# The last block's head reordered: a short first route, one query unit in two row buffers, one output unit's slot for rows

## The reference, cut to what matters

```python
h = rmsnorm(x, norm1_g) * (1 + sc1) + sh1
q, k, v, u = split(h @ w_in)
mixed = concat([dilated_attention(q, k, v), multiscale_pool(u)]) @ w_out
x = x + g1 * mixed
h2 = rmsnorm(x, norm2_g) * (1 + sc2) + sh2
x = x + g2 * peer_ffn(h2)
return rmsnorm(x, final_g)

def peer_ffn(h):                       # 8 heads, 2 x 128 sub-keys, 16384 experts
    q = h @ w_q                        # 1024 -> 8 heads x 2 x 128
    s = q . sub_keys                   # two times 128 scores for each token and head
    sv, si = top_k(s, 16)              # the 16 best of each half
    cand = sv[0][:, None] + sv[1]      # 256 sums, with id = 128 * si[0] + si[1]
    top_v, eid = top_k(cand, 16)
    gate = softmax(top_v)
    act = gelu(h . expert_u[eid])
    return sum(gate * act * expert_v[eid])
```

## Time and profile before

| what | us |
|---|---|
| median of 3 runs | 1417.58 |
| lowest, highest | 1414.52, 1530.66 |
| the profiled execution's own time | 1416.4 |
| its span, first to last instruction | 1414.6 |
| busy: PE, DVE, POOL, ACT | 1277.5, 818.0, 651.8, 412.3 |

### The profile page before, as it was taken

The page is one execution under the profiler, slowest core; times in us unless marked ns, Lnnn a source line. Parts: engine busy times, 40 slices in busy tenths (PEclk is TensorE's granted clock), DMA queues, the critical chain, the costliest instruction groups (busy, mean ns, idle before and its releaser), DMA issues.

```text
span 1414.6 us, 17530 instructions
## 1 busy us (share of the span) xinstructions
PE 1277.5 (90%) x6312; PEld 788.6 (56%) x6312; DVE 818.0 (58%) x1681; ACT 412.3 (29%) x1030; POOL 651.8 (46%) x643
## 2 busy tenths in 40 slices
PE   9999999999999999999998899958967888777786
PEld 8887686548886777559566556523323333333332
DVE  1766287340666377350448756889797654554545
ACT  1533334201342333121314323332313231212123
POOL 0556667423446766504004354535645455454540
PEclk9999999999999999999999999979999989999999
DMA  9544344634444254543628999999999999999995
GB/s 373 206 164 180 120 165 168 262 131 183 164 180 173 96 233 177 195 176 141 271 86 329 421 417 415 421 421 421 421 421 421 421 423 421 422 422 421 422 421 209
DMA packets 53888, 407.84 MB, mean 288 GB/s; under 512 B 6165, under 2 KB 8618, under 8 KB 11306
## 3 DMA queue, kind: packets, MB, share of 16 engines
q0 software_dynamic: 36864, 268.45, 45.9%
q1 hardware_dynamic: 15850, 137.23, 25.2%
q10 hardware_dynamic: 1088, 1.05, 0.3%
HBM read 404.58 MB, written 1.07 MB: 287 GB/s over the span
## 4 chain that ended last, share of the span: by engine, by line
PE 28%; DMA 24%; DVE 6%; issue 3%; ACT 2%; POOL 1%; ACTq 0%; DVEq 0%; POOLq 0%
PE bank L1119 10%; DMA ring<-in_peer_uv,vM 7%; DMA yT<-in_peer_uv,vM 7%; PE pj L729 6%; PE pj L693 4%; DMA hv<-in_peer_uv,vM 4%; DMA more_rows<-in_peer_uv,vM 3%; DMA qM<-in_peer_uv,vM 3%; PE pj L989 2%; PE pj L708 2%; DVE tri L1871 1%; DMA qvE<-in_peer_uv,vM 1%; PE bank L999 1%; ACT rope L1338 1%; DVE big L1871 1%
## 5 line engine op out<-in xcount | busy, mean ns | idle before, releaser
L693 PE MATMUL pj<-xT,ring 128*128 128x256 f32 (+1 forms) x1568 | 318.4, 363 | 0.9 <-ACT hv L1276 0.4
L693 PEld LDWEIGHTS pj<-xT,ring 128*128 128x128 f32 x1568 | 276.6, 190 | 36.5 <-issue 2.6
L607 POOL TENSOR_SCALAR more_rows<-more_rows,lbt 128x256 f32<-128x256 f32 x168 | 176.0, 1048 | 16.4
L641 POOL DMA_INDIRECT ring<-in_peer_uv,vM x101 | 122.5, 1213 | 120.9 <-PE bank L1119 109.5
L729 PE MATMUL pj<-ring,yT 128*128 128x512 f32 x320 | 141.1, 595 | 0.0
L605 POOL TENSOR_SCALAR mod_part<-more_rows,lbt 128x256 f32<-128x256 f32 x24 | 23.7, 989 | 246.6 <-issue 122.1
L1336 ACT ACTIVATE rope<-vM 128x4 f32<-128x4 f32 (+3 forms) x84 | 17.1, 204 | 405.6 <-DVE big L1871 323.0
L608 POOL TENSOR_TENSOR mod_part<-mod_part,more_rows 128x256 f32<-128x256 f32 x168 | 127.9, 761 | 14.0
L1119 PE MATMUL bank<-ring,causal 128*128 128x512 f32 x200 | 99.9, 638 | 19.2 <-ACT causal L1344 19.2
L1119 PE MATMUL bank<-ring,tri 128*128 128x512 f32 x204 | 99.4, 627 | 19.4 <-ACT tri L1344 19.4
L729 PEld LDWEIGHTS pj<-ring,yT 128*128 128x128 f32 x320 | 59.7, 190 | 69.5 <-issue 69.2
(11 more groups left out here) (369 smaller groups left out, 2114.0 us busy)
## 6 DMA issues: line engine op xcount, KB each, us to landing
ring<-in_units SPq DMA_DIRECT2D x44, 2048.0 KB, 9.5
more_rows<-in_w_ada SPq DMA_DIRECT2D x24, 1024.0 KB, 4.9
ring<-in_units SPq DMA_DIRECT2D x2, 1536.0 KB, 7.8
ring<-in_peer_uv,vM POOLq DMA_INDIRECT x101, 23.1
memT<-in_mem SPq DMA_DIRECT2D x2, 512.0 KB, 5.3
ring<-in_units SPq DMA_DIRECT2D x1, 1024.0 KB, 9.0
xT<-in_x_turned SPq DMA_DIRECT2D x1, 1024.0 KB, 10.7
x<-in_x SPq DMA_DIRECT2D x1, 1024.0 KB, 16.0
```

Of the source, the lines that this page charges most:

```text
L607: do(g.tensor_scalar(mod_w[:, c, :], mod_w[:, c, :], silu_c[:, c:c + 1], None, ALU.mult))
L641: pool.indirect_dma_start(row_slot[k], None, d["peer_uv_2"], bass.IndirectOffsetOnAxis(ap=expert[:, t, j:j + 1], axis=0))\
L693: ins = nc.tensor.matmul(pj[s][0:n, 2 * m + first:2 * m + stop], ring[:, slot, at:at + n], act[:, c, first:stop], start=(c == 0), stop=(c ...
```

## The change

It changes the last block alone.

- The order of PE: the first half of O1 for tile u (`O1v`), `Zt`, `K0at` and `E0t` come before the last attention tasks of tile u; `O1w`, `O0v` and `O0w` follow them. Rows (`W`) are spread in smaller steps among the query pieces. ACT and DVE follow suit.
- `half_norm` of tile t is cut in two tasks, `OMta` and `OMtb`.
- A first route `Ra` takes the top 8 of both halves of head 0, straight from PSUM, and finds its first 8 picks among 8 x 8 sums. Eight gathers can start with them. `Rt0` then does the rest of head 0, and `XP1` only its last 8 ids.
- The H2 rows for the dots are no longer made by DVE: PE transposes `xT` back (`Ht`, `Hu`), ACT copies it. So two of the four modulation rows need not be loaded, and the gate row moves from `hv` to `big`, so that `hv` is free from the start.
- K1 is loaded into two row buffers (`more_rows` and `kM`), once the last attention scores are done, in place of the ring. The ring slot of O1 takes rows instead, from row 0 on. The slots' order and the rows from which they take part change.
- Four PSUM uses get fixed banks.

```diff
-            """Xt BUt BKt Xu MT BUu BKu BQa BQb SK S0 S1 BVa S2 PL0 PL1 BVb P0 P1 S3 S4 Y0 S5 Y1 O1t P2 O0t P3 Y2 P4 Y3 P5 Y4
-            Y5 O1u Zt O0v K0at E0t O0w K0bt E1t K1at Zu K1bt E2t K0au W4 K0bu E3t W5 W7 EU0 K1au W11 K1bu W15 EU1 W21
-            K20 W27 K21 W31 K22 W32 K23 W36 E4 W37 E5 W40 K30 W42 K31 W45 K32 W49 K33 W55 E6 E7 W256"""]
+            """Xt BUt BKt Xu MT BUu BKu BQa BQb SK S0 S1 BVa S2 PL0 PL1 BVb P0 P1 S3 S4 Y0 S5 Y1 O1t P2 O0t P3 O1v Zt Y2 P4
+            K0at Y3 E0t P5 Y4 Y5 O1w O0v Ht O0w K0bt W9 E1t W11 K1at K1bt W19 Zu W20 W21 E2t W22 E3t W23 K0au W24 K0bu
+            W27 K1au K1bu EU0 W29 K20 W31 W32 Hu W33 W38 W39 W40 K21 W41 W42 W43 K22 EU1 W44 K23 W45 W46 E4 W47 E5 W48
+            K30 W49 W50 W52 K31 W53 W54 W55 K32 K33 W56 W58 E6 W60 W63 W64 W65 E7 W256"""]
-ACT_LAST = """Xu BU BK BQa BQb SK S0 S1 MT S2 BV P0 P1 S3 S4 P2 S5 P3 P4 P5 OMt Zt K0at E0t T1 K0bt E1t OMu Zu K1bt W1
...
+ACT_LAST = """Xu BU BK BQa BQb SK S0 S1 MT S2 BV P0 P1 S3 S4 P2 S5 OMta OMtb P3 Zt K0at P4 P5 E0t T1 Ht W2 W3 K0bt W8 W9 W10
+    E1t W11 OMu W12 K1bt W13 W14 W15 T2 W17 W18 W19 W20 W21 Zu W22 E2t W23 W24 W25 W26 W27 E3t K0bu W29 EU0 W30 W31
...
-DVE_LAST = """Xu S0 S1 S2 PL0 PL1 N0 N1 S3 N2 S4 S5 N3 N4 Y1 N5 OMt Y5 NMt Zt Rt0 XP1 OMu H2t NMu D1 Zu D3 H2u D4 GT1
-    D5 Rt1 D8 XP2 D9 Rt2 D15 Rt3 D16 GT2 D18 XP3 D37 GT3 D44 Rt4 D50 Rt5 D54 XP4 D62 GT4 D63 Rt6 Rt7 D72 XP5
...
+DVE_LAST = """Xu S0 S1 S2 PL0 PL1 N0 N1 S3 N2 S4 S5 N3 N4 Y1 N5 OMt NMt Zt Ra Y5 Rt0 XP1 D3 GT1 D7 OMu D11 Rt1 XP2 D17 D18 GT2
+    D19 NMu D22 D23 Zu D24 D25 D26 Rt2 D28 Rt3 XP3 D31 D34 D35 GT3 D36 D40 D51 D52 Rt4 D53 D54 Rt5 D55 D56 D57 D58
+    XP4 D60 D62 D64 D66 D67 Rt6 GT4 D71 D72 Rt7 D74 D76 XP5 D77 D78 D81 GT5 D83 D84 Ru0 Ru1 Ru2 Ru3 D89 XP6 D104 GT6
...
-NEW_SLOTS = {0: ("", range(0, 7)), 18: ("K1", (7, 8)), 41: ("K2", (9, 10)), 67: ("K3", (11, 12, 13)), 74: ("E7", (14,))}
+NEW_SLOTS = {0: ('', (2, 3, 6, 4, 5, 7, 8)), 33: ('K1', (0, 1)), 52: ('K2', (9, 10)), 66: ('K3', (11, 12, 13)), 92: ('E7', (14,))}
...
+                if STREAM[n] == (B2, "K1"):
+                    sp.wait_ge(sem("scores2"), 6)
+                    for g, rows in enumerate(spare_rows):
+                        load(rows, d["units"][n, :, g * 2 * D_MODEL:(g + 1) * 2 * D_MODEL], "spare_load")
+                    return
...
-            starts = part_starts()
+            starts = {0: 1, TOPK // 2: 2, **{n: part + 1 for n, part in part_starts().items() if n}}
...
+                elif k in (0, 1):
+                    unit_done(pool, B2, "K1")
                 elif k in (2, 3):
                     pool.wait_ge(sem("y2_ready"), 2)
                 elif k in (4, 5):
                     unit_done(pool, B2, OUT_UNITS[B2][-1])
-                elif k == 6:
-                    pool.wait_ge(sem("h2_ready"), TT)
...
+                elif k > 6:
+                    unit_done(pool, B2, ("O1", "O1", "K2", "K2", "K3", "K3", "K3")[k - 7])
...
+                elif name in ("Ht", "Hu"):
+                    tile = "tu".index(task[1])
+                    after(pe, "xT_ready", l - 1, 2 * tile + 5)
+                    for j in range(2):
+                        key = (l, ("H", 2 * tile + j))
+                        transposes(key, [(bank_of(key)[:, c * P:(c + 1) * P], xT[:, 4 * j + c, tile * P:(tile + 1) * P])
+                                         for c in range(4)])
...
+                        if task == "E0t":
+                            act.wait_ge(sem("first_read"), 1)
...
+            def first_route():
+
+                n, top = TOPK // 2, cand[:, 0:TOPK // 2 * (TOPK // 2)]
+                key = (l, ("E0t",))
+                bank_filled(dve, key)
+                halves = [(bank_of(key)[:, k * P:(k + 1) * P], sub_val[:, 0, 0, k, 0:n], sub_id[:, 0, 0, k, 0:n]) for k in range(2)]
+                for scores, values, ids in halves:
+                    do(v.max(values, scores), behind=1)
+                do(v.max_index(halves[0][2], halves[0][1], halves[0][0]), behind=1)
+                do(v.max_index(halves[1][2], halves[1][1], halves[1][0]), "first_read")
...
+                do(v.max(top_val[:, 0, 0, 0:n], top))
+                do(v.max_index(top_pos[:, 0, 0:n], top_val[:, 0, 0, 0:n], top))
+                chosen(0, 0, slice(0, n), n, 3)
...
+                    if j == 0:
+                        dve.wait_ge(sem("h2_ready"), 2 * (t + 1))
...
-                    do(v.tensor_tensor(normed[:, t, :], normed[:, t, :], row_scale2, ALU.mult))
-                    do(v.tensor_tensor(normed[:, t, :], normed[:, t, :], row_shift2, ALU.add), "h2_ready")
```

More of the change, by code:

```diff
@@ L233, in bank_index @@
             few = few or (l == B2 and task == "Zt")
+            if l == B2 and task == "Y2":
+                use((l, ("AO", 1)), BANK_FIXED["AO", 1])
             for key in bank_uses(l, task):
-                use((l, key), n % 2 if few else n % 4)
+                if l == B2 and key == ("AO", 1):
+                    out[l, key] = (n, *out[l, key][1:])
+                    n += 1
+                    continue
+                if l == B2 and key in BANK_FIXED:
+                    use((l, key), BANK_FIXED[key])
+                elif few:
+                    use((l, key), turn % 2)
+                    turn += 1
+                else:
+                    use((l, key), n % 4)
                 n += 1
@@ L975, in expert_queries @@
             def expert_queries(name, columns, tiles):
-                if name == "K2":
-                    pe.wait_ge(sem("aside_load"), 32)
-                    w = [rows.rearrange("p (c n) -> p c n", c=DC // 2)[:, c, :] for rows in aside for c in range(DC // 2)]
+                if name in ("K1", "K2"):
+                    homes, landed = {"K1": (spare_rows, "spare_load"), "K2": (aside, "aside_load")}[name]
+                    pe.wait_ge(sem(landed), 32)
+                    w = [rows.rearrange("p (c n) -> p c n", c=DC // 2)[:, c, :] for rows in homes for c in range(DC // 2)]
                 else:
@@ L1347, in expert_weights, with half_norm @@
                 assert n0 == last
-            def half_norm(t, ready, spare):
+            def half_norm(t, ready, spare, halves=range(2)):
                 sums, part = stat[:, 16 + 2 * t:18 + 2 * t], stat[:, 20 + t:21 + t]
-                for half in range(2):
+                for half in halves:
                     c = slice(half * COLS, (half + 1) * COLS)
@@ L1368, in _ @@
                     transposed_x(l, "Z", (0,) if name == "Zt" else (2,), modc[:, 4, :], modc[:, 3, :])
+                elif name in ("Ht", "Hu"):
+                    t = "tu".index(task[1])
+                    for j in range(2):
+                        key = (l, ("H", 2 * t + j))
+                        bank_filled(act, key)
+                        do(a.copy(normed[:, t, j * COLS:(j + 1) * COLS], bank_of(key)[:, :]), *bank_free(key))
+                        act.sem_inc(sem("h2_ready"), 1)
                 elif task == "MT":
@@ L1411, in _ @@
                     t = "tu".index(task[2])
-                    half_norm(t, "x_mid", pT_of if t else [flat_pair[:, 0:COLS], flat_pair[:, COLS:]])
+                    half_norm(t, "x_mid", pT_of if t else [flat_pair[:, 0:COLS], flat_pair[:, COLS:]],
+                              {"": range(2), "a": (0,), "b": (1,)}[task[3:]])
                 elif task in ("K0at", "K0bt", "K1bt"):
@@ L1944, in _ @@
                     if t == 0:
[L1945 removed]
+                        dve.wait_ge(sem("mod_rows_load"), 32)
                     else:
```

91 lines of the change are left out of this document (56 added, 35 removed).

## The result

The changed kernel takes 1406.63 us in the median of 4 runs (1405.63 to 1407.71), the kernel before 1414.52 beside it on the same chip (1413.33 to 1417.58; a fourth execution, in a slower state, took 1530.66 and is left out). The ratio is 0.9936, with a 95% interval from 0.9917 to 0.9954: a gain of 0.5 to 0.8%, 6.5 to 11.7 us, so nothing that counts as faster by 2%. The profiled execution took 1405.63 us for a span of 1403.8, 10.8 less than the 1416.4 and 1414.6 of before. The forecast was 1405.5, and its range 1397 to 1417.

The account below looks back on a forecast made before the run. The gather stream at 421 GB/s was taken as the bound: start, constant, losses. Starting 12.4 us earlier less 1.6 more lost gives 10.8, say 11, off 1416.4: 1405.5 us forecast, range 1397 to 1417.

Parts of the forecast that it names:

- What bounds the kernel: Second half of the kernel: stream start, bytes at 421 GB/s, losses and a 12.4 us tail fix the end.
- The head: Work before the first gather: the new order and shorter first route issue it 12.4 us earlier, between 9 and 14.
- The wait at row 16: Row 16's gather waits for ids from XP2, behind D11 and Rt1: loss 0 to 3 us, taken 1.
- The wait at rows 32 and 33: Row 32 needs ids from XP3, at 820.5 to 825: loss 0 to 5 us, taken 3.5; row 33 needs K1bu.
- in time, with 2 to 5 us to spare: PE's query pieces K1bu, K23 and K33 end at 819, 866, 901, before rows 33, 52, 66 need their slots.
- Small gaps: Along the gather stream: another 1.5 us of loss.
- K1's load, "nothing": Moving K1's load from 724.84 to the last attention scores, before 713, was to cost or gain nothing.
- O1's slot for rows: Seven row slots at the start are 17.4 us of stream, giving slack of some 10 us.
- Losses eat it: Rival: expert waits at rows 16, 32 and 64 each cost some 3 us more; gain 2, 1412 to 1418; chance 0.20.
- PE becomes the bound: Rival: at row 33 POOL waits for K1bu, which comes at 837 to 840; 1425 us; chance 0.07.
- The head does not move: Rival: Zt or E0t is held, first gather at 737, gain 5, 1411 us; chance 0.05.
- The page of the skill: First three gathers, beside Rt0 and XP1, could each take the longer issue time; about 1 us less gain.

Follow-up runs that it names:

- E0t: Not a run: a PE step of the kernel, after K0at and before the first route; no time of its own is given.
- gelu_first: Changed kernel with ACT loading the gelu table right after tile u's row norm; 1407.16 us, ratio 0.9930.
- tuned: Changed kernel with ids of rows 32 on sooner, O0w before Ht, K23 before EU1 and a row group, gelu table loaded early; 1404.17 us, ratio 0.9915.
- tuned2: tuned plus the spread routes of ru_spread, XP4 two dots sooner, and K32, K33 earlier on PE; 1406.09 us, ratio 0.9924.
- E3t: Not a run: a short group of score matmuls on PE; with two other score groups and the transposes Zu some 2.2 us together.
- pe_pad: Changed kernel with PE computing query piece K1au twice, 3.6 us more work ahead of row 33; 1407.84 us, ratio 0.9946.
- ru_spread: Changed kernel with tile u's first four routes set apart by four rows' dots each, instead of back to back; 1405.04 us, ratio 0.9926.
- the two K1 runs: Changed kernel with K1 back in O1's ring slot and rows given more_rows and kM, in two slot orders; 1411.92 us and 1411.55 us.

## Why the prediction was right, point by point

The forecast was "11 us give or take 5". The profiled executions differ by 10.8; the ratios of the two batches make it 9 and 10. The sum's 10.8 met the profile's 10.8 by luck: the start gave 12.9 and not 12.4, the losses took 3.5 and not 1.6, which makes 9.4. The other 1.4 lie in what the table calls the rest, whose scatter is 2, and are not explained.

*What bounds the kernel* held: start, bytes at 421 GB/s, losses, tail. (The rates read as "415 to 424" are 415 to 423 in the earlier trace rows.) The check in the prediction ends at 1394.3, 8 us before the last dot, and calls the rest the queue's drain. In the trace of before the rate falls to 66 GB/s from 1395 on and the last rows are still dotted one by one, 2.46 to 2.49 us apart, until 1402.24; in that of after it falls to 75 from 1385 on, and the last dot is at 1391.40. So the drain is there, about 6 us in both, and cancels.

*The head* held to 1.1 us at each step. `Zt` was put at 716.8 and ran at 716.22; `K0at` 719.9 and 719.38; `Ra` 725.4 and 724.89, so 5.51 us from `K0at` to it where 5.5 was taken. `Ra` was taken at 4.2 between the bounds 2.5 and 7.8, and took 3.6. The ids were put at 729.6 and came at 728.51, 1.1 sooner; the first gather came at 730.25, 12.9 us earlier where 12.4 was forecast. The rest of that 1.1 went to `Y5`'s copy, for which the first gather waits and which the prediction had put at no loss. The fourth was put at 739.6 and issued at 738.82, and its hole is 1.8 us where 1.3 was taken.

*The wait at row 16* is the term that was mis-sized. `XP2`'s ids were put at 772.2 and ended at 772.27. The loss was taken as 1 and measured as 2.6. The walk stopped at the ids. Behind them the dots that had piled up come out one by one, and the first needs ACT for its weight. ACT had just used another function and loads a table for 1.28 us. ACT of the changed kernel:

```profile
774.04 1.28 ACT L1366 ACT_TABLE_LOAD   x1 [3.68 <-DVE big L1953]
```

So row 18, which needs that row's slot, stood until 778.61. `gelu_first` shows that this load was 1.3 us of the way between rows 16 and 18. That the loss of the stream shrinks with it is seen in `tuned` (1.7) and `tuned2` (2.0), not in `gelu_first` itself (3.7).

*The wait at rows 32 and 33* was put at "820.5 to 825" with a loss of 3.5; it was 821.56 and 2.7. The prediction said that POOL's idle at row 33 would be ended by K1's matmuls: wrong, it was ended at row 32 by the ids. PE was close behind.

*PE* "in time, with 2 to 5 us to spare" is the step that failed. `K1bu` was put at 819 and ended at 822.3; `K23` at 866 and ended at 871.3. The first cost nothing because the ids were as late. The second held row 52 until 871.71 and lost 1.0. `K33` was put at 901 and ended near 906, where row 66 went at 906.20 behind it, at no loss. It was not the idling that was missed: PE stood 7.8 us up to 822.3 and 10.1 up to 871.3, where the walk had 8. It was the work. From 738.39 on PE was busy some 76 us up to 822.3, where 27 rows at 1.72 and 7 pieces at 3.45 make 70.6. Four short groups between them (the scores `E1t`, `E2t`, `E3t` and the transposes `Zu`, some 2.2 us together) are not in these durations, a K1 piece took 3.57, and the matmuls of a row that stands singly 1.88 to 1.98 and not 1.72. `pe_pad` shows that what comes on top of it shows.

*Small gaps*, 1.5, were not spread about as thought. Two holes of 1.0 and 1.2 stand for them; the first is `K23`'s, and that near 1000, of four routes back to back, was not foreseen and is shown by `ru_spread` and again by `tuned2` (421 GB/s in both, 406 to 414 in the ten other profiles of the new order).

Losses so come to 9.2 and not 7.3. Of the 1.9 more, 0.5 is set against the earlier start.

*K1's load, "nothing"*, held against the kernel before, where the unit was out of the stream too. But it is no idle edit. With the head this early, K1 in the ring would have gone out with the first rows and cost 5.0 us as bytes, and 7 in all. This part of the change is worth about as much as the early ids.

*O1's slot for rows* the prediction only used, as the reason why there is "slack of some 10 us". It goes together with K1's move: K1 takes two of the seven slots of before for a while, and O1's ring slot gives two back. Without these two the kernel is 21 us slower, and slower than before; against before the pair is worth the 5 to 7 us of the two K1 runs.

*hv's freedom and the H2 rows by PE* were not tried alone. That hv waits for nothing is seen at 732.97.

*The rivals.* "Losses eat it" had the right direction and 3.5 of its 10.6 us. "PE becomes the bound" at row 33 did not come, but was half a microsecond away. "The head does not move" fell with 730.25.

*The page of the skill.* The trace shows the first three gathers issued in 1.18, 0.94 and 0.94 us beside `Rt0` and the start of `XP1`. The Trainium skill, SBUF — State Buffer, section "Who interferes with whom", names copies, casts and tensor_scalar; here the longer time did not come. But this was hardly a test: up to 732.6 VectorE ran MAX8, FIND_INDEX8, MATCH_REPLACE8 and tensor_tensor, and the third gather alone stood beside casts and tensor_scalars, of 0.3 us and less. Issues of 1.9 to 2.0 us occur later, as at row 52 (1.92); all are under the 2.49 us of a row.
